# Decay attention, one head behind the other, with its projections in three fp32r passes placed between the heads' work

## The chip, the cores and the metric

One core of one Trainium2 chip runs the whole program. The metric is the device time of one launch in microseconds (us), as the median of several runs. TensorE (PE, with its weight loads as PEld) does the matmuls, VectorE (DVE) and ScalarE (ACT) the elementwise work, GpSimd (POOL) and SyncE (SP) help; each engine takes its own instructions in order, and waits on semaphores that the others raise.

## What is computed

The program is a small network on 512 tokens of width 1024: two layers of a first kind (two feed-forward blocks and a mixer each), then a second block with sparse attention, a mixture of experts, decay attention ("hgrn") and a second mixture of experts. The change touches decay attention alone. Of the reference, cut:

```python
def hgrn2_mixer(h, lower_bound, w_in, out_gain, w_out):
    q, f, i, g = jnp.split(h @ w_in, ...)             # 1024 columns each
    q = jax.nn.silu(q)                                # 8 heads of 128 keys
    log_f = log(lb + (1 - lb) * sigmoid(f));  k = 1 - exp(log_f);  v = i
    def chunk_step(S, xs):
        cum = jnp.cumsum(lf_c, axis=2)
        rel = where(causal, cum[t] - cum[s], -inf)
        attn = einsum('bhtd,bhsd,bhtsd->bhts', q_c, k_c, exp(rel))
        o = attn @ v_c + (q_c * exp(cum)) @ S
        S = exp(last) * S + (k_c * exp(last - cum))^T @ v_c
    o = rms_norm(o, out_gain) * jax.nn.silu(g)
    return o @ w_out
```

`x` becomes `x + gate * y`, with `h` the modulated norm of `x`.

## The kernel before

`P` is 128, `TT` 4 token tiles of 128, `KT` 8 tiles of the width, `HG` 8 heads. The stage (`hgrn`, L1631 on) opens with `Norm`: statistics of `x`, 32 transposes on PE, and eight evacuations shared by ACT and DVE into `hT`. It is in plain fp32, 4 MB of SBUF tiles hold all heads at once, and the phases run for all heads before the next phase begins:

- Projections of forget gates and queries (L1720): 16 tiles of 512 columns, eight matmuls each, in six PSUM banks (`Banks`). The weights come through `Ring`, two slots of 2 MB, and go to PE as they are. ACT and DVE evacuate (`evacuate`, L595 and L597); DVE scales the gates (L1875 to L1877), ACT takes the logarithm (L1820), DVE the running sums over 128 tokens (L1881), ACT the silu of the queries.
- Levels. The causal 128x128 square of each head and token tile is put together from eight patterns: the diagonal, and for each block size 1, 2, ... 64 the pairs in which the key is in the first and the query in the second half of a block of twice that size. Such a unit (head, size) is: two subtractions on DVE (`gaps`, L1893 and L1894, 256 columns each), an exponential on ACT (L1828), two multiplications by keys and queries on DVE (L1902, L1903), four 128x128 matmuls on PE (L1744) and a predicated copy into `att` on DVE (L1910). There are 64 units; those of the diagonals come first. PE's order puts one tile of the value and gate projections (L1729, eight matmuls) ahead of every four units. The decayed product has four slots (`M`), a level two PSUM banks.
- States and outputs: key decays for all heads (L1919, L1836, L1924), 32 transposes of keys (L1753), query decays (L1928), then by token tile the state increments (L1774), the states (L1947, L1953) and the outputs (L1781, L1785), their squares (L1936, L1937).
- The end: root, normalisation and gate (L1965, L1967), 32 transposes (L1793), evacuation with the gain, and the output projection (L1807, 64 matmuls), whose results are added to `x` (L1080, L1081).

Other stages of the same program already use three passes in fp32r, a rounded format: `split_matmul` (L209 to L213) multiplies high by high, high by low and low by high parts. A weight half of 1 MB is split by ACT (the high part, a copy to fp32r, as L2180 in the experts stage) and DVE (the low part, a subtraction, L2268), and `ModulatedSplitNorm` (L250) splits `h` in the same way.

Of the kernel before, what the change touches and what calls it, by code (L numbers as in the profile page):

```python
# [1630 lines left out]
def hgrn(chip):  # L1631
# [5 lines left out]
    units = [(h, None) for h in range(HG)] + [(h, b) for h in range(HG) for b in LEVELS[1:]]  # L1637
    U = len(units)
    with Scope(nc, "hgrn") as s:
        banks = Banks(s, 6)  # L1640
        level_ps = [s.ps(f"level{i}", [P, SEQ]) for i in range(2)]

        FQ, VG, KK, GROW, OC, OT, OUT = 0, 16, 32, 40, 42, 50, 58
        a = s.sb("region_a", [P, 4096])
        b = s.sb("region_b", [P, 4096])
        norm = Norm(chip, s, banks.ps[0:4], a[:, :], b[:, :])
        norm.allocate(s)
        qT = s.sb("qT", [P, HG, SEQ])
        kT = s.sb("kT", [P, HG, SEQ])
        cum = s.sb("cum", [P, HG, SEQ])  # L1650
        v = s.sb("v", [P, TT, DM])
        g = s.sb("g", [P, TT, DM])
        scratch = a[:, :].rearrange("p (h t) -> p h t", h=HG)
        att = b[:, :].rearrange("p (h c t) -> p h c t", h=HG, c=TT)
        kk = a[:, :].rearrange("p (c d) -> p c d", c=TT)
        o_tok = cum[:, :, :].rearrange("p h t -> p (h t)").rearrange("p (c d) -> p c d", c=TT)
        o_heads = cum[:, :, :].rearrange("p h t -> p (h t)").rearrange("p (u e) -> p u e", e=P)
        squares = kT[:, :, :].rearrange("p h t -> p (h t)").rearrange("p (u e) -> p u e", e=P)
        cum_ch = cum[:, :, :].rearrange("p h t -> p (h t)").rearrange("p (u t) -> p u t", t=P)
        counts = [4, 8, 12, 16, 20, 24, 28, 32, OUT + 4, OUT + 8]  # L1660
        ring = Ring(s, 2, [(dram["hgrn_w"][i], 4096, n) for i, n in enumerate(counts)], banks.computed)
        masks = s.sb("masks", [P, len(LEVELS), P], I32)
        keep = s.sb("keep", [P, SEQ])
        M = [s.sb(f"decayed{i}", [P, SEQ]) for i in range(4)]
        state = [s.sb(f"state{i}", [P, HG, P]) for i in range(2)]
# [3 lines left out]
        gate_row = s.sb("gate_row", [P, DM])  # L1669
        diag = s.sb("diag", [P, KT, P])  # L1670
        small_loaded, own_v = s.sem("small_loaded"), s.sem("own_v")
        lb_diff, lb_exp = s.sem("lb_diff"), s.sem("lb_exp")
        f_scaled, f_log, q_silu, g_silu, cum_ready = s.sem("f_scaled"), s.sem("f_log"), s.sem("q_silu"), s.sem("g_silu"), s.sem("cum_ready")
        gaps_ready, decays_ready, m_ready = s.sem("gaps_ready"), s.sem("decays_ready"), s.sem("m_ready")
        level_done, level_taken, att_zeroed = s.sem("level_done"), s.sem("level_taken"), s.sem("att_zeroed")
        cum_exp, last_gaps, last_exp, q_decayed, k_decayed = s.sem("cum_exp"), s.sem("last_gaps"), s.sem("last_exp"), s.sem("q_decayed"), s.sem("k_decayed")
        decay_ready, state_done, state_ready = s.sem("decay_ready"), s.sem("state_done"), s.sem("state_ready")
        o_var, o_rstd, o_normed, diag_ready, x_added = s.sem("o_var"), s.sem("o_rstd"), s.sem("o_normed"), s.sem("diag_ready"), s.sem("x_added")
        block = s.block()

        outputs = {}
        for m in range(HG):
            outputs[FQ + 2 * m] = [piece(cum[:, m, :], func=ACT.Sigmoid), piece(kT[:, m, :], func=ACT.Sigmoid, scale=-1.0)]
            outputs[FQ + 2 * m + 1] = [piece(qT[:, m, :])]
            outputs[KK + m] = [piece(kk[:, m // 2, 512 * (m % 2):512 * (m % 2) + 512])]
            outputs[OC + m] = [piece(o_tok[:, m // 2, 512 * (m % 2):512 * (m % 2) + 512])]
            outputs[OT + m] = [piece(qT[:, m, :], scale=chip.gain("hgrn_out_gain_2", 0))]
# [24 lines left out]
        def _(pe):  # L1712
# [10 lines left out]
            for step in range(16):  # L1723
# [8 lines left out]
                for u in range(4 * step, 4 * step + 4):  # L1732
# [8 lines left out]
                    if u >= 2:  # L1741
                        pe.wait_ge(level_taken, u - 1)
# [988 lines left out]
```

## Time and profile before

| | us |
|---|---|
| median of 3 runs (3726.86 to 3735.7) | 3733.4 |
| profiled execution | 3737.17 |
| its span | 3735.2 |
| decay attention in it, 2891.3 to 3354.0 | 462.7 |

Busy over the whole span: PE 3360.6 us (90%), PEld 2599.2, DVE 2025.7 (54%), ACT 1338.0 (36%), POOL 159.2 (4%). The table says that PE is the busiest engine overall, but one stage among many is changed, and what bounds that stage must be read from its own windows: how long each phase takes, how much of it PE, DVE and ACT are busy, and which engine's records stand ahead of the idle time. A busy share below 100% on every engine at once means that they wait for each other in turn.

### The profile page before, as it was taken

The page shows a single profiled execution, that of the slowest core. Times are in us where ns is not written, and L with a number is a line of the kernel's source. Part 1 is how long each engine was busy: PE and PEld are TensorE (multiplying, and loading weights), DVE is VectorE, ACT ScalarE, POOL GpSimd, SP SyncE. Part 2 cuts the span into 40 slices and gives each one's busy share as a digit, 9 for nine tenths or more (in the row PEclk, how much of TensorE's full clock was granted, in tenths as well). Part 3 has the DMA queues.
Part 4 walks back from the last instruction along what each step waited for, and adds up shares of the span by engine and source line. Part 5 has one row for each costly group of instructions (what it writes and reads, how often), then busy time and mean ns, then how long its engine had stood idle before and what let it go on. Part 6 is the DMA issues. An engine that isn't in the chain of part 4 may idle for free. (4 is left out here: it accounts for less than half of the span.)

```text
span 3735.2 us, 39164 instructions
## 1 busy us (share of the span) xinstructions
PE 3360.6 (90%) x15110; PEld 2599.2 (70%) x15110; DVE 2025.7 (54%) x2724; ACT 1338.0 (36%) x1734; POOL 159.2 (4%) x194
## 2 busy tenths in 40 slices
PE   7999988999989999888999798888996988778995
PEld 6888756788878887567888585457885444547884
DVE  4554435555455544255554544545987246746886
ACT  3222223322132222243222323635885121305884
POOL 0000000000000000000000003410100000000100
PEclk9999999999999999999999797997998999997998
DMA  4331320433143323304331411017995210107995
GB/s 187 152 128 63 128 102 1 180 136 134 56 161 140 133 73 118 112 1 163 152 135 56 146 46 68 1 51 294 415 415 228 90 68 23 46 22 276 415 415 228
DMA packets 85490, 537.55 MB, mean 144 GB/s; under 512 B 9232, under 2 KB 10128, under 8 KB 37088
## 3 DMA queue, kind: packets, MB, share of 16 engines
q1 hardware_dynamic: 72912, 489.95, 33.9%
q0 software_dynamic: 7824, 28.84, 2.0%
q10 hardware_dynamic: 4608, 16.78, 1.1%
q8 instruction: 95, 1.56, 0.2%
q14 instruction: 51, 0.42, 0.0%
HBM read 512.43 MB, written 32.02 MB: 146 GB/s over the span
## 5 line engine op out<-in xcount | busy, mean ns | idle before, releaser
L211 PE MATMUL ffn_gate_up<-ffn_h_high,ffn_gate_up_high 128*128 128x512 f32 x1408 | 548.4, 389 | 7.1 <-DVE ffn_h_low L245 7.1
L213 PE MATMUL ffn_gate_up<-ffn_h_high,ffn_gate_up_low 128*128 128x512 f32 x1408 | 548.0, 389 | 0.0
L212 PE MATMUL ffn_gate_up<-ffn_h_low,ffn_gate_up_high 128*128 128x512 f32 x1408 | 547.9, 389 | 0.0
L2268 DVE TENSOR_TENSOR moe_low<-moe_raw,moe_high 128x2048 fp32r<-128x2048 f32 x192 | 433.9, 2287 | 38.6 <-ACT moe_high L2180 38.4
L451 ACT ACTIVATE ffn_silu_gate<-ffn_gate_up 128x512 f32<-128x512 f32 x88 | 52.7, 598 | 971.6 <-PE ffn_gate_up L213 971.6
L2180 ACT ACTIVATE moe_high<-moe_raw 128x2048 fp32r<-128x2048 f32 x192 | 364.4, 1917 | 18.9 <-PE moe_bank L213 18.9
L482 DVE TENSOR_TENSOR ffn_product<-ffn_silu_gate,ffn_gate_up 128x512 f32<-128x512 f32 x88 | 60.5, 688 | 568.8 <-ACT ffn_silu_gate L451 568.8
L211 PEld LDWEIGHTS ffn_gate_up<-ffn_h_high,ffn_gate_up_high 128*128 128x128 f32 x1408 | 264.3, 188 | 63.2 <-DVE ffn_h_low L245 8.4
L213 PEld LDWEIGHTS ffn_gate_up<-ffn_h_high,ffn_gate_up_low 128*128 128x128 f32 x1408 | 264.3, 188 | 55.2
L212 PEld LDWEIGHTS ffn_gate_up<-ffn_h_low,ffn_gate_up_high 128*128 128x128 f32 x1408 | 264.3, 188 | 55.1
L506 DVE SCALAR_TENSOR_TENSOR x_tok<-ffn_down,x_tok 128x512 f32<-128x512 f32 x352 | 232.9, 687 | 94.6 <-PE ffn_down L213 93.2
L211 PE MATMUL ffn_down<-ffn_down_high,ffn_hid_high 128*128 128x512 f32 x704 | 282.5, 401 | 1.6 <-DVE x_tok L506 1.6
L212 PE MATMUL ffn_down<-ffn_down_low,ffn_hid_high 128*128 128x512 f32 x704 | 281.0, 399 | 0.0
L213 PE MATMUL ffn_down<-ffn_down_high,ffn_hid_low 128*128 128x512 f32 x704 | 280.6, 399 | 0.0
L470 DVE TENSOR_TENSOR ffn_gate_up_low<-ffn_raw_gate_up,ffn_gate_up_high 128x2048 fp32r<-128x2048 f32 x88 | 201.5, 2289 | 74.1 <-ACT ffn_gate_up_high L440 74.0
L211 PE MATMUL moe_bank<-moe_high,moe_xT_high 128*128 128x512 f32 x512 | 207.0, 404 | 4.3 <-DVE moe_xT_low L2275 4.3
L213 PE MATMUL moe_bank<-moe_high,moe_xT_low 128*128 128x512 f32 x512 | 201.2, 393 | 0.0
L212 PE MATMUL moe_bank<-moe_low,moe_xT_high 128*128 128x512 f32 x512 | 200.8, 392 | 0.0
L440 ACT ACTIVATE ffn_gate_up_high<-ffn_raw_gate_up 128x2048 fp32r<-128x2048 f32 x88 | 168.2, 1912 | 39.8 <-DMA ffn_raw_gate_up<-in_ffn_gate_up 39.8
L211 PEld LDWEIGHTS ffn_down<-ffn_down_high,ffn_hid_high 128*128 128x128 f32 x704 | 135.0, 192 | 33.6 <-DVE x_tok L506 2.4
L213 PEld LDWEIGHTS ffn_down<-ffn_down_high,ffn_hid_low 128*128 128x128 f32 x704 | 134.7, 191 | 32.0
L212 PEld LDWEIGHTS ffn_down<-ffn_down_low,ffn_hid_high 128*128 128x128 f32 x704 | 135.0, 192 | 31.2
(488 smaller groups left out, 5645.2 us busy)
## 6 DMA issues: line engine op xcount, KB each, us to landing
moe_raw<-in_moe_w SPq DMA_DIRECT2D x192, 1024.0 KB, 7.8
ffn_raw_gate_up<-in_ffn_gate_up SPq DMA_DIRECT2D x88, 1024.0 KB, 6.5
ffn_ada_w<-in_ada_w SPq DMA_DIRECT2D x32, 1536.0 KB, 6.6
ffn_raw_down<-in_ffn_down SPq DMA_DIRECT2D x88, 512.0 KB, 3.3
mixer_w_raw<-in_mix_w SPq DMA_DIRECT2D x24, 1024.0 KB, 5.2
hgrn_ring<-in_hgrn_w SPq DMA_DIRECT2D x10, 2048.0 KB, 7.6
moe_y<-moe_y ACTq DMA_DIRECT2D x32, 512.0 KB, 9.4
nsa_w_raw<-in_nsa_w SPq DMA_DIRECT2D x14, 1024.0 KB, 5.3
```

Of the source, the lines that this page charges most:

```text
L211: pe.matmul(out, lhsT[0], rhs[0], start=first, stop=False)
L212: pe.matmul(out, lhsT[0], rhs[1], start=False, stop=False)
L213: return pe.matmul(out, lhsT[1], rhs[0], start=False, stop=last)
L440: act.activation(gu_high[slot][:, :, :, :], raw_gu[slot][:, :, :, :], ACT.Copy).then_inc(gu_high_ready, 1)
L451: act.activation(silu_gate[slot][:, :], gate_up_ps[2 * slot][:, :], ACT.Silu).then_inc(silu_done, 1)
L470: dve.tensor_tensor(gu_low[slot][:, :, :, :], raw_gu[slot][:, :, :, :], gu_high[slot][:, :, :, :].bitcast(FP32), ALU.subtract).then_inc(gu ...
L482: dve.tensor_tensor(product[slot][:, :], silu_gate[slot][:, :], gate_up_ps[2 * slot + 1][:, :], ALU.mult)\
L506: dve.scalar_tensor_tensor(out=xs, in0=down_ps[o % 4][:, :], scalar=0.5, in1=xs, op0=ALU.mult, op1=ALU.add).then_inc(x_added, 1)
L2180: act.activation(high[n % SPLITS][:, :, :], raw[n % RAWS][:, :, :], ACT.Copy).then_inc(high_ready, 1)
L2268: dve.tensor_tensor(low[n % SPLITS][:, :, :], raw[n % RAWS][:, :, :], high[n % SPLITS][:, :, :].bitcast(FP32), ALU.subtract)\
```

## The change

The stage is written anew, with the same mathematics:

- All projections, those of the output too, go by `split_matmul`. `h` is split by `ModulatedSplitNorm`. Each of the 20 halves of weights (1 MB) is loaded into one of two raw buffers, split by `make_high` on ACT and `make_low` on DVE into one of two pairs. Matmuls of 128x512: 320 in fp32 before, 960 in fp32r now. A `part` is the work of one half of the contraction (four of eight tiles) for one bank: 12 matmuls. Four banks are open per group of 512 columns.
- Units are ordered head by head. The first two groups (values of heads 0 to 3; gates and queries of heads 0 and 1) are projected ahead; then 72 ticks follow, and 48 parts of the next six groups are spread over the first 64 of them, none in every fourth. In tick n each engine's program has: `gaps(n)`, `multiply(n-1)`, `keep_level(n-3)` on DVE, `decays(n)` on ACT, at most one part and `level(n-2)` on PE. Per head, from tick 8h+8 on, come query and key decays, three transposes of keys, three state increments, the states and the outputs; the sums of squares are taken by ACT (four `Square` with accumulation). At given ticks `make_high`, `make_low`, the gates, silus, logarithms and scans of later heads are put in.
- `gaps` is one subtraction of 512 columns instead of two of 256, `multiply` one product of 512 instead of two, `decays` two exponentials of 256 (one with scale -1) instead of one of 512. `M` has three slots, not four.
- At the end, normalisation and gate are one operation for each head and tile (32 of 128 columns); each token tile is transposed, split by ACT and DVE, and its first part of the output projection may start when that tile is ready.

```diff
-    units = [(h, None) for h in range(HG)] + [(h, b) for h in range(HG) for b in LEVELS[1:]]
+    units = [(h, b) for h in range(HG) for b in LEVELS]
+    GROUPS = [("v", 0), ("fq", 0), ("fq", 1), ("fq", 2), ("v", 1), ("fq", 3), ("g", 0), ("g", 1), ("out", 0), ("out", 1)]
+    FIRST, PARTS = 2, 48
+    def tick_of(part):
+        return -(-(part + 1) * U // PARTS) - 1
...
-            ring.fill(sp, 0, 2)
+            for n in range(2 * len(GROUPS)):
+                if n >= 2:
+                    sp.wait_ge(w_ready, n - 1)
+                sp.dma_start(raw[n % 2][:, :], dram["hgrn_w"][COLUMNS[kind] + i, :, ...]).then_inc(w_loaded[n % 2], 16)
...
-                    for k in range(KT):
-                        last = pe.matmul(bank[:, :], w[:, k, m * P:(m + 1) * P], norm.hT[:, k, :], ...)
+            def part(gi, half, m):
+                if m == 0:
+                    pe.wait_ge(w_ready, n + 1)
+                if half == 0 and gi >= 1:
+                    pe.wait_ge(taken[m], gi)
+                if kind == "out" and gi == len(GROUPS) - 2 and half == 0:
+                    pe.wait_ge(oT_ready, 2 * m + 2)
+                for i in range(4):
+                        last = split_matmul(pe, banks[m][:, :], ...)
...
+            for tick in range(U + 8):                                      # TensorE
+                while p < PARTS and tick_of(p) <= tick:
+                    part(FIRST + p // 8, p // 4 % 2, p % 4)
+                if 0 <= tick - 2 < U:
+                    level(tick - 2)
+                h, at = divmod(tick - 8, 8)
+                    if at == 2: turn_keys(h)
+                    if at == 4: increments(h)
+                    if at == 6: output(h)
...
+            for tick in range(U + 8):                                      # ScalarE
+                    decays(tick)
+                    if n + 2 < 20 and tick == done_tick(n // 2, n % 2, 3) + 1: make_high(n + 2)
+                        if tick == done_tick(gi, 1, 2) + 1: forget_gates(gi)
+                        if tick == done_tick(gi, 1, 3) + 1: queries(gi)
+                        if tick == done_tick(gi, 1, 3) + 3: logs(i)
+                if at == 7: query_decay(h + 1)
+                    if at == 1: key_decay(h)
+                    if at == 3: take_keys(h)
+                    if at == 7: take_output(h)
+                if tick == U + 2:
+                        act.activation(g[:, t, :], g[:, t, :], ACT.Silu)
...
+            for tick in range(U + 8):                                      # VectorE
+                    gaps(tick); multiply(tick - 1); keep_level(tick - 3)
+                    if at == 0: query_decay(h)
+                    if at == 1: key_decay(h)
+                    if at == 5: add_states(h)
+                    if n + 2 < 20 and tick == done_tick(n // 2, n % 2, 3) + 2: make_low(n + 2)
...
+            def gaps(u):
+                if w >= 3:
+                    dve.wait_ge(level_done, 8 * ((w - 3) // 7) + (w - 3) % 7 + 2)
...
+            for t in range(TT):
+                for h in range(HG):
+                    dve.scalar_tensor_tensor(out=o_tok[:, t, h * P:(h + 1) * P], ..., op0=ALU.mult, op1=ALU.mult).then_inc(o_normed, 1)
+                if t > 0:
+                    take_turned(t - 1)
```

## Rows read from the trace of the kernel before

**Rows 1.** Busy time by stretch of the stage: length, busy of each engine, clock, DMA.

```profile
2891.30:2904.90 13.60, 6.72 (x32) 5.91 (x32) 9.66 (x19) 8.96 (x13) 0.84 (x1) 0.57 0.92 364
2904.90:3014.90 110.00, 109.95 (x257) 48.76 (x258) 18.12 (x36) 14.49 (x25) 2.67 (x1) 1.00 0.16 58
3014.90:3236.60 221.70, 179.46 (x769) 111.12 (x767) 141.44 (x308) 46.64 (x75) 0.00 (x0) 0.98 0.13 48
3236.60:3281.00 44.40, 27.82 (x208) 27.12 (x208) 37.40 (x69) 21.59 (x33) 0.00 (x0) 0.81 0.00 1
3281.00:3354.00 73.00, 62.27 (x160) 30.25 (x160) 23.57 (x28) 2.75 (x4) 0.00 (x0) 0.91 0.00 0
```

**Rows 2.** The ring's matmuls: records, ns min/median/max, first and last start (us), forms.

```profile
L1720 PE MATMUL hgrn_bank<-hgrn_region_a,hgrn_ring x256: 592/592/667, 2904.9 to 3014.5; 128*128 128x512 f32 x128
L1729 PE MATMUL hgrn_bank<-hgrn_ring,hgrn_region_a x256: 592/592/1061, 3014.9 to 3229.5; 128*128 128x512 f32 x128
L1807 PE MATMUL hgrn_bank<-hgrn_ring,hgrn_qT x128: 592/592/667, 3297.3 to 3351.9; 128*128 128x512 f32 x128
```

**Rows 3.** Timeline, experts stage, fp32r passes: start (us), us, engine, line, operation.

```profile
2850.24 0.39 PE L211 MATMUL moe_bank<-moe_high,moe_xT_high 128*128 128x512 f32 x1
...
2852.73 0.39 PE L213 MATMUL moe_bank<-moe_high,moe_xT_low 128*128 128x512 f32 x1
```

**Rows 4.** Timeline of one period in the levels: start (us), us; brackets hold idle and releaser.

```profile
3069.92 7.03 PE L1729 MATMUL hgrn_bank<-hgrn_ring,hgrn_region_a 128*128 128x512 f32 x16
...
3076.79 1.95 PE L1744 MATMUL hgrn_level<-hgrn_decayed 128*128 128x128 f32 x16
3077.88 0.73 DVE L1910 COPY_PREDICATED hgrn_region_b<-hgrn_masks,hgrn_level 128x512 f32<-128x512 int32 x1 [4.61 <-PE hgrn_level L1744]
...
3083.42 7.03 PE L1729 MATMUL hgrn_bank<-hgrn_ring,hgrn_region_a 128*128 128x512 f32 x16
```

**Rows 5.** Groups by line (L1445: sparse attention): busy us, mean ns, idle, releaser.

```profile
L1910 DVE COPY_PREDICATED hgrn_region_b<-hgrn_masks,hgrn_level 128x512 f32<-128x512 int32 x64 | 46.4, 725 | 76.1 <-PE hgrn_level L1744 76.0
L1903 DVE TENSOR_TENSOR hgrn_decayed<-hgrn_decayed,hgrn_qT 128x256 f32<-128x256 f32 x56 | 23.8, 426 | 1.9
L1928 DVE TENSOR_TENSOR hgrn_qT<-hgrn_qT,hgrn_decayed 128x512 f32<-128x512 f32 x8 | 4.9, 681 | 0.0
L1953 DVE SCALAR_TENSOR_TENSOR hgrn_state<-hgrn_state,hgrn_decay,hgrn_level 128x128 f32<-128x128 f32 x16 | 4.4, 343 | 0.8 <-PE hgrn_level L1774 0.6
L1828 ACT ACTIVATE hgrn_decayed<-hgrn_decayed 128x512 f32<-128x512 f32 x56 | 35.3, 630 | 169.3 <-DVE hgrn_decayed L1894 169.3
L1781 PE MATMUL hgrn_bank<-hgrn_v,hgrn_region_b 128*128 128x128 f32 x64 | 11.7, 284 | 0.0
L1445 ACT ACTIVATE nsa_k_tok<-nsa_k_tok,nsa_neg_max 128x256 f32<-128x256 f32 x32 | 16.0, 500 | 10.4 <-DVE nsa_neg_max L1585 10.4
```

**Rows 6.** The splits of the experts' weight halves: count, ns min/median/max, first and last start.

```profile
L2180 ACT ACTIVATE moe_high<-moe_raw x192: 1897/1915/1932, 2531.1 to 3685.2; 128x2048 fp32r<-128x2048 f32 x192
L2268 DVE TENSOR_TENSOR moe_low<-moe_raw,moe_high x192: 2280/2285/2295, 2545.0 to 3687.2; 128x2048 fp32r<-128x2048 f32 x192
```

**Rows 7.** Timeline: ACT changes its function table ahead of the gate's silus.

```profile
3257.86 1.28 ACT L1844 ACT_TABLE_LOAD   x1
3259.16 3.90 ACT L1844 ACTIVATE hgrn_g<-hgrn_g 128x1024 f32<-128x1024 f32 x4
```

**Rows 8.** Timeline, sparse attention stage: its split norm, and a projection after idle time.

```profile
2098.51 1.89 ACT L712 ACTIVATE nsa_w_high<-nsa_w_raw 128x2048 fp32r<-128x2048 f32 x1
...
2109.34 0.77 PE L211 MATMUL nsa_bank<-nsa_h_high,nsa_w_high 128*128 128x512 f32 x1
...
2464.28 0.76 PE L211 MATMUL nsa_bank<-nsa_w_high,nsa_oT_high 128*128 128x512 f32 x1 [4.86 <-issue]
...
2469.50 0.40 PE L211 MATMUL nsa_bank<-nsa_w_high,nsa_oT_high 128*128 128x512 f32 x1
```

**Rows 9.** DMA issues: count, KB each, median us from issue to landing.

```profile
hgrn_ring<-in_hgrn_w SPq DMA_DIRECT2D x10, 2048.0 KB, 7.6
```

More of the change, by code:

```diff
@@ L1639, in hgrn @@
     with Scope(nc, "hgrn") as s:
-        banks = Banks(s, 6)
+        banks = [s.ps(f"bank{i}", [P, 512]) for i in range(4)]
         level_ps = [s.ps(f"level{i}", [P, SEQ]) for i in range(2)]
[L1643 to L1649, printed above, removed]
@@ L1661, in hgrn @@
-        ring = Ring(s, 2, [(dram["hgrn_w"][i], 4096, n) for i, n in enumerate(counts)], banks.computed)
-        masks = s.sb("masks", [P, len(LEVELS), P], I32)
+        att = s.sb("att", [P, 2, TT, P])
+        M = [s.sb(f"decayed{i}", [P, SEQ]) for i in range(3)]
+        kk = s.sb("kk", [P, TT - 1, P])
+        state = s.sb("state", [P, TT - 1, P])
+        decay_of = s.sb("decay_of", [P, SEQ])
+        squares = s.sb("squares", [P, P])
+        masks = s.sb("masks", [P, len(LEVELS) - 1, P], I32)
@@ new lines, in level @@
+            def level(u):
+                h, size = units[u]
+                if size is None:
+                    pe.wait_ge(cum_ready, h + 1)
+                    left, right = k_of(h), q_of(h)
+                else:
+                    pe.wait_ge(m_ready, index(h, size) + 1)
+                    left = right = slot(u)
+                if u >= 2:
+                    pe.wait_ge(level_taken, u - 1)
+                for c in range(TT):
+                    last = pe.matmul(level_ps[u % 2][:, tokens(c)], left[:, tokens(c)], right[:, tokens(c)], start=True, stop=True)
+                last.then_inc(level_done, 1)
@@ L1788, in _ @@
[L1788 to L1809 removed]
+                last.then_inc(row_done, 1)
@@ new lines, in queries, with logs @@
+            def queries(gi):
+                pair = GROUPS[gi][1]
+                for i in range(2):
+                    h, m = 2 * pair + i, 2 * i + 1
+                    act.wait_ge(computed, 4 * gi + m + 1)
+                    if h >= 4:
+                        act.wait_ge(o_done, h - 3)
+                    act.activation(q_of(h), banks[m][:, :], ACT.Silu).then_inc(taken[m], 1)
+            def logs(pair):
+                for h in range(2 * pair, 2 * pair + 2):
+                    act.wait_ge(f_scaled, h + 1)
+                    act.activation(cum[:, h % 4, :], cum[:, h % 4, :], ACT.Ln).then_inc(f_log, 1)
```

599 lines of the change are left out of this document (353 added, 246 removed).

## The prediction

> **What bounds the kernel now.** The rest of the program is untouched, so only the stage's 462.7 us can move. I read it by stretches first [rows 1]: norm 13.6 us, gate and query projections 110.0, levels with the value and gate projections 221.7, key decays to the outputs' statistics 44.4, end 73.0. Their PE column is the thing to see: PE is busy 109.95 of 110.0 in the second stretch and 179.5 of 221.7 in the third, so matmul time is the limit there, with 42.2 us of waiting on top. In the fourth PE is busy 27.8 of 44.4 with DVE at 37.4: there DVE leads. In the fifth 62.3 of 73.0 is PE again, after a serial normalisation.
>
> Then the size of the matmul work. 128 matmuls of 128x512 (256 records) run from 2904.9 to 3014.9 [rows 1, 2], 0.859 us each. All 320 are 275 us of the 462.7. In the experts stage the same shape in fp32r starts at 2850.24 and, eleven matmuls later, at 2852.73 [rows 3]: 0.2264 us, thus 0.679 for three passes. (The 0.39 us in the row is duration and overlaps the next.)
>
> Then how the third stretch loses its 42 us. A period runs from one projection tile to the next, 3069.92 to 3083.42, 13.5 us; within it PE does eight matmuls in one go (7 us) while DVE, having used up its four slots, stands idle 4.6 us; then PE waits for DVE's products [rows 4]. DVE's idle time before the predicated copies is 76.0 us in all, released by PE [rows 5]. Both engines wait in turn.
>
> **The change part by part.** The sum follows PE from 2891.3 on.
>
> *Norm and first split, 13.6 becomes 18.4.* ACT now splits a weight half before it evacuates, and each of the eight tiles of `h` costs DVE two operations in a row instead of one in every second tile. The sparse attention stage has the same chain: from its first weight split (2098.51) to its first projection matmul (2109.34) 10.8 us [rows 8]. The split starts when the weights have landed; the two first halves are 2 MB together, which took 7.6 us [rows 9]. Statistics, memset and masks hide below it. 7.6 + 10.8 = 18.4, bounds 15 and 21.
>
> *The first two groups, 45.* 16 parts of 12 matmuls: 192 x 0.2264 = 43.5. After idle time the first 12 matmuls of a projection took 5.22 us (2464.28 to 2469.50) instead of 2.72 [rows 8], so up to 2.5 more; I take 1.5. Weight splits are hidden: a half costs ACT 1.92 and DVE 2.29 [rows 6], 4.2 in sequence, and must be ready one half of PE work (10.9 us) after its buffer is freed. The SP queue waits for `w_ready` before each load, with only later loads behind it. Then PE has parts for tick 1 to 3 but waits for the first scan and product behind logarithms, splits and table loads: 2.
>
> *The 64 ticks, PE's own work 213.* 48 parts are 576 x 0.2264 = 130.4. A level is half of the 1.95 us that 16 records take [rows 4], 0.98; 62 of them until the last part are 61. Per head 13 more 128x128 matmuls: at the levels' 0.245 they are 3.2, at the 0.37 of the output matmuls (11.7 us for 32, [rows 5], partly at the low clock) 4.8; seven heads, near the first, 22. Semaphore switches between parts and levels are in the waiting below.
>
> *DVE beside it, about 180.* Before, a unit cost four operations of 256 columns (0.42 to 0.43) and a copy of 0.73. Now it is two of 512, 0.68 each [rows 5] with about 0.08 of overlap, and the copy: about 1.85, for 64 units some 115 with the diagonals left out. The shape of `multiply` (two strided runs in one access) is in no row; from 0.68 up to the two old operations, 0.85; I take 0.68, the row of its element count. Twelve low splits add 27, per head query and key decays and three states (three at 0.68, three at 0.34, plus own waits) 3.2, thus 24 for seven and a half heads; gates, scans and takes of the six later groups 20. Near 83% of PE's 213. *ACT beside it, about 140.* Two exponentials of 256: the row of that width has 0.50 with two accumulations and a pointer, half of the 512 one is 0.32 [rows 5]; I take 0.4, 45 in all; high splits 23, gates and takes 18, per head decays, squares and the output copy 4.5, 34; table changes 23. Two thirds of 213.
>
> *Table changes.* The old order needs seven or eight in the stage, the new one six per group of gates in the loop (sigmoid, exponential, silu, exponential, logarithm, exponential), 18 more. One took 1.28 us, the next activation began 1.30 after its start [rows 7]: 23 us. They stand in the ticks where a high split and six gate activations stand too. The Trainium skill ("ScalarE: Activation LUTs", section "What ACT_TABLE_LOAD costs") gives 2.66 us for a change, a drain of 1.38 included, and tells to batch activations by table set, which this change undoes. By that figure ACT would have 25 us more, which its third of free time still covers in the mean; the sum would rise by at most 12 where they bunch. The trace has no room for the drain (1.30), so the row is taken.
>
> *What waits and what is queued behind it.* A level on PE waits for the product of its unit, and the next part is queued behind it; `gaps` waits until the slot three units back was read by PE, with DVE's copies and splits behind. Each engine may therefore be about one tick ahead. A PE tick is 3.7 with a part and 1.0 without, 3.3 in the mean with the heads; DVE's is 1.85, but 4 to 5.7 where a low split and gate scaling fall in it, ACT's 0.8, but 4.5 and 6.5 in the two ticks in a row where gates and queries come. `queries` of head 5 waits for `output(1)`, at the end of its own tick on PE, with the next exponentials behind. I give 3 us per group of gates (9), and 0.7 per low split (8): 17, 8% of 213. Bounds: 0 (every burst covered), and 42, what PE idles in this stretch now [rows 1].
>
> *From the last part to the root, 44.4 becomes 18.* The phases over eight heads are gone; what is left is head 7: two levels 2, decays 2 (largely beside them), but the gate's silus (1.3 + 3.9, [rows 7]) now stand ahead of ACT's copy of the turned keys, 5.2; copy 0.5, increments 0.7, states 1.3, outputs 1.7, four squares and a copy 2.6, statistics and root with a table load 2; waits and low clock 2. Bounds 15 and 24.
>
> *The end, 73.0 becomes 54.* Before, everything was normalised and turned before the first of 64 x 0.859 = 55 us. Now a tile's eight operations of 128 columns (0.28 to 0.34, [rows 5]) are 2.5; with transposes, split and the next tile's normalisation between, the first part starts after 6.2, the following 3.7 apart, the fourth, whose banks are freed last, after 16. Then its own 2.7, 12 parts of 2.72 (32.6), two additions 1.6, slow start 1. The splits of the last two halves (4.2 each) fit in 10.9. Bounds 51 and 59.
>
> Sum: 18.4 + 45 + 2 + 213 + 17 + 18 + 54 = 367.4, against 462.7: 95.3 less. The span 3735.2 becomes 3639.9, the profiled time 3737.2 becomes 3641.9; the median of the runs stands 3.8 below the profiled time, so the median is 3733.4 - 95.3 = 3638.1.
>
> **The rivals.**
>
> *Forecast, 0.60:* PE sets the pace with a moderate loss, 3638, own range 3626 to 3650.
>
> *Every burst is covered, 0.14:* DVE has 17% and ACT a third of slack. No waiting in the ticks: 3621. Against it: three engines in fixed order with a lead of one tick.
>
> *They still wait in turn, 0.19:* the bursts hit harder, and PE loses the 42 us that it loses now, 25 more than in the sum: 3663. For it: DVE's 83% leaves little room to catch up, and unmeasured shapes may be dearer (multiply at 0.85 adds 10 us of DVE). In stretches with more idle PE time the granted clock was 0.81 [rows 1], the lower of two levels (1.2 and 2.4 GHz) for part of it, which makes waiting dearer.
>
> *Slower, 0.04:* one lap of the ring of slots sets each tick. With three slots instead of four, a unit's gaps 0.68, exponentials 0.8, product 0.68, the part ahead of its level 2.7, level 0.98 and copy 0.73 come one after the other, 6.6 us a tick; 62 ticks are 409 instead of 230, the median 3817. It decides from 5.2 us a tick on (3.7 + 95/62). Against it: slots for three units allow three such chains at once, a lap of 6.6 thus 2.2 per unit, below PE's tick.
>
> *Nothing gained, 0.03:* the three passes don't run at 0.2264 here or ticks come to 5.0 to 5.4 by some mix. Were a pass a third of 0.859, it would cost 57 us more, 3695; only with slow ticks besides it comes to no change.
>
> **How the numbers follow.** About 0.3% (11 us) is what a measurement of this kernel can tell from no change. The first three cases are faster: 0.60 + 0.14 + 0.19, and half of the last one's 0.03 with a little: 0.94. Same 0.02, slower 0.04. The range must leave out at most 2 in 10: it takes the second and third case with the bounds of norm, tail and end (about 8 either way): 3621 - 8 = 3613, 3663 + 9 = 3672.
>
> **What the profile would show.** Matmuls of the projections at 0.226 us from start to start, 960 of them. Right: 64 ticks in 225 to 235 us, PE over 88% busy there, DVE 75 to 85%, the stage 360 to 375 us. The wait view should name DVE's `multiply` (level waits) ahead of `computed` waits; ACT with some 26 table loads. The first projection matmul near 18 us from the start, the last part to the root near 18, the end near 54. Wrong would be: ticks over 4.2 us in the mean, DVE over 95% busy (then its new shapes cost more), a copy or exponential that holds PE for over 5 us in each group, or a clock below 0.9 in the loop.

## The result and the profile after

The changed kernel takes 3638.8 us in the median (3633.2 to 3647.2), the kernel before 3731.5 in runs on the same chip: 0.9754 of its time, 95% interval 0.9731 to 0.9776. The forecast was 3638. In a later series it took 3639.2 (0.9738, interval 0.9720 to 0.9755). The profiled execution of the changed kernel has a span of 3637.2 us.

The stage now runs from 2886.9 to 3253.3 us of the span, 366.4 us against 462.7 before [rows 1]; 367.4 were forecast. These are the stretches of the changed kernel that answer to [rows 1]: norm and first split, first two groups, ticks up to the last part, up to the statistics' root, up to the first part of the output projection, and the rest. Columns: stretch, length, busy time and number of instructions of PE, weight loads, DVE, ACT and POOL, granted clock, DMA share, GB/s.

```profile
2886.90:2905.10 18.20, 8.30 (x32) 6.12 (x33) 15.09 (x25) 12.15 (x16) 0.00 (x0) 0.50 0.60 213
2905.10:2950.50 45.40, 45.40 (x191) 36.72 (x190) 18.50 (x25) 13.74 (x13) 0.95 (x1) 0.97 0.29 93
2950.50:3172.50 222.00, 212.33 (x1230) 184.29 (x1229) 175.45 (x260) 130.55 (x271) 0.00 (x0) 0.98 0.18 58
3172.50:3191.70 19.20, 10.71 (x64) 9.24 (x62) 9.41 (x14) 12.13 (x23) 0.00 (x0) 0.73 0.17 55
3191.70:3205.20 13.50, 6.63 (x32) 5.58 (x33) 12.44 (x38) 5.40 (x9) 0.00 (x0) 0.62 0.00 0
3205.20:3253.30 48.10, 46.54 (x194) 37.10 (x192) 17.06 (x20) 4.77 (x4) 0.00 (x0) 0.97 0.00 0
```

PE is busy 96% of the ticks, against 81% of the third stretch of [rows 1], with DVE at 79% and ACT at 59%. What PE still waits for in the ticks (engine, tile and line, released by; us in total, times, longest):

```profile
PE hgrn_kk_bank L1791 <- ACT hgrn_kk L1909: 5.9, 3, 2.7
PE hgrn_level L1777 <- DVE hgrn_att L2036: 1.4, 2, 0.8
PE hgrn_bank L211 <- ACT hgrn_kq L1872: 1.1, 1, 1.1
PE hgrn_bank L211 <- ACT hgrn_kq L1881: 0.9, 1, 0.9
PE hgrn_level L1777 <- DVE hgrn_decayed L2026: 0.3, 1, 0.3
```

These are 9.6 us, all that the ticks' row leaves beside PE's busy time (222.0 - 212.3). The groups of instructions (busy us, mean ns, idle before them and its releaser), for the copies, products, gaps and exponentials of [rows 5]:

```profile
L2036 DVE COPY_PREDICATED hgrn_att<-hgrn_masks,hgrn_level 128x512 f32<-128x512 int32 x56 | 41.4, 739 | 9.7 <-PE hgrn_level L1777 9.7
L2026 DVE TENSOR_TENSOR hgrn_decayed<-hgrn_decayed,hgrn_kq 128x512 f32<-128x512 f32 x56 | 38.3, 684 | 0.7 <-ACT hgrn_decayed L1893 0.7
L2019 DVE TENSOR_TENSOR hgrn_decayed<-hgrn_cum 128x512 f32<-128x512 f32 x56 | 38.2, 684 | 24.9 <-PE hgrn_level L1777 24.9
L1892 ACT ACTIVATE hgrn_decayed<-hgrn_decayed 128x256 f32<-128x256 f32 x56 | 23.8, 425 | 89.6 <-DVE hgrn_decayed L2019 89.5
```

The product over two strided runs takes 684 ns, as its element count said. The 76 us that DVE idled before its copies in [rows 5] are 9.7 now, with 24.9 more before the gaps.

The same program profiled once more (`changed_again` below) has the ticks in 219.0 us at a granted clock of 1.00 instead of 222.0 at 0.98, and the stage in 363.4. PE's list of waits is the same in both, to within 0.1 us, so all 3 us are PE's busy time (209.3 against 212.3). Stage lengths are therefore compared with 363.4 to 366.4, and a difference under 3 us is not read unless the clocks are equal.

### The profile page after: what moved, and what is told of

Its sections match the earlier page's. It is cut to its first block and busy times, and to the rows that moved or that the text cites. A ratio compares the mean times of both kernels' runs of the same rounds, so it can differ in the third digit from the quotient of the medians.

```text
span 3637.2 us, 40038 instructions
## 1 busy us (share of the span) xinstructions
PE 3302.4 (91%) x15422; PEld 2651.7 (73%) x15422; DVE 2043.3 (56%) x2647; ACT 1421.7 (39%) x1916; POOL 156.5 (4%) x194
```

## The experiments

| kernel | median us (range) | ratio to before, 95% | stage us | ticks us | PE busy in ticks |
|---|---|---|---|---|---|
| changed kernel | 3638.8 (3633.2–3647.2) | 0.9754 (0.9731–0.9776) | 366.4 | 222.0 | 212.3 |
| e1_parts_between | 3624.8 (3621.0–3629.1) | 0.9715 (0.9693–0.9738) | 358.4 | 219.1 | 209.4 |
| e2_fp32 | 3681.5 (3676.1–3683.4) | 0.9862 (0.9836–0.9889) | 406.6 | 241.9 | 239.4 |
| e3_two_passes | 3585.8 (3582.3–3589.5) | 0.9607 (0.9582–0.9633) | 319.7 | 203.4 | 178.3 |
| e4_more_dve | 3657.3 (3656.9–3662.8) | 0.9807 (0.9780–0.9833) | 377.5 | 232.3 | 214.4 |
| e5_two_slots | 3690.1 (3686.6–3693.9) | 0.9876 (0.9860–0.9893) | 424.1 | 275.7 | 229.4 |
| e5_four_slots | 3634.3 (3630.9–3638.0) | 0.9733 (0.9717–0.9750) | 363.1 | 219.0 | 210.8 |
| e6_layout | 3642.3 (3638.5–3649.3) | 0.9758 (0.9739–0.9776) | 366.1 | 221.8 | 212.1 |
| e8_keys_first | 3629.9 (3628.9–3636.6) | 0.9722 (0.9704–0.9741) | 359.4 | 215.4 | 208.4 |
| changed_again | 3639.2 (3629.2–3640.6) | 0.9738 (0.9720–0.9755) | 363.4 | 219.0 | 209.3 |
| e7_aligned | 3629.9 (3626.4–3630.6) | 0.9719 (0.9704–0.9733) | 361.9 | 219.1 | 208.6 |
| e9_all | 3622.1 (3614.1–3625.2) | 0.9697 (0.9681–0.9714) | 346.5 | 212.3 | 206.1 |
| e10_all_and_down | 3613.0 (3596.5–3622.0) | 0.9684 (0.9668–0.9701) | 346.6 | – | – |

Edits are against the changed kernel. The kernel before stood at 3731.5 us beside the first row, and at 3733.0, 3733.3 and 3733.8 beside the three series of four kernels that follow, each on one chip. Only `e7_aligned`, `e9_all` and `e10_all_and_down` have the changed kernel (`changed_again`) in their own series. The medians of the others are set beside the first row, from another chip, and are the weaker figure (14 us less in the first experiment, where its stage is 5 to 8 shorter).

**The end: parts between the transposes.** Of the terms of the sum only the end fell outside its bounds: 13.5 + 48.1 = 61.6 us against 54 (51 to 59). The timeline of the changed kernel, PE and DVE from the first normalisation on (start, us, engine, line, operation, in brackets idle time before it and releaser), shows why:

```profile
3193.95 0.66 PE L1840 MATMUL hgrn_kk_bank<-ident,hgrn_o_tok 128*128 128x128 f32 x4 [2.54 <-DVE hgrn_o_tok L2145]
...
3196.57 0.74 DVE L2139 SCALAR_TENSOR_TENSOR hgrn_oT_low<-hgrn_o_bank,cols,hgrn_oT_high 128x512 fp32r<-128x512 f32 x1
3196.80 1.09 PE L1840 MATMUL hgrn_kk_bank<-ident,hgrn_o_tok 128*128 128x128 f32 x4 [1.67 <-DVE hgrn_oT_low L2139]
...
3200.22 1.09 PE L1840 MATMUL hgrn_kk_bank<-ident,hgrn_o_tok 128*128 128x128 f32 x4 [1.48 <-DVE hgrn_oT_low L2139]
...
3203.64 1.09 PE L1840 MATMUL hgrn_kk_bank<-ident,hgrn_o_tok 128*128 128x128 f32 x4 [1.47 <-DVE hgrn_oT_low L2139]
3204.52 1.06 PE L1840 MATMUL hgrn_o_bank<-ident,hgrn_o_tok 128*128 128x128 f32 x4
...
3205.23 0.78 PE L211 MATMUL hgrn_bank<-hgrn_w_high,hgrn_oT_high 128*128 128x512 f32 x1
```

The operands of the first part are split at 3197.31 (3196.57 and 0.74), yet it starts at 3205.23: in PE's program the transposes of all four tiles stand ahead of it, 3.4 us apart from the second tile on, each pair waiting for DVE's low half. Putting the parts between them is the experiment.

```diff
+            last_group = len(GROUPS) - 2
             for t in range(TT):
...
                     last.then_inc(o_turned, 1)
-            for gi in range(len(GROUPS) - 2, len(GROUPS)):
-                for half in range(2):
-                    for m in range(4):
-                        part(gi, half, m)
+                if t > 0:
+                    part(last_group, 0, t - 1)
+            part(last_group, 0, TT - 1)
+            for m in range(4):
+                part(last_group, 1, m)
+            for half in range(2):
+                for m in range(4):
+                    part(last_group + 1, half, m)
```

> The changed kernel, with one edit at its end: on TensorE the first half part of the output projection for token tile t-1 is queued right behind the transposes of tile t, instead of all four behind the transposes of all four tiles. In the profile of the changed kernel the first part starts 13.5 us after the first normalisation (3191.7 to 3205.2) and the projection takes 48.1 us, 61.6 in all; the sum had 54, with parts from 6.2 us on. Theory (PE's own queue order was mis-read: parts stand behind the last tile's transposes): the first part moves to about 7 us and the two stretches together to 53 to 56, so 6 to 8 us less than the changed kernel, about 3631. Rival (the low clock after the idle stretch and VectorE's pace of 3.4 us a tile eat it): the parts run at 0.43 us a matmul between the transposes and delay these; 60 us or more in all, less than 2 us gained.

The end of the experiment's kernel:

```profile
3191.50:3198.20 6.70, 2.68 (x16) 2.47 (x17) 6.68 (x23) 2.68 (x5) 0.00 (x0) 0.76 0.00 0
3198.20:3248.00 49.80, 48.22 (x210) 38.94 (x208) 22.82 (x36) 7.28 (x8) 0.00 (x0) 0.96 0.00 0
```

The first part starts 6.7 us after the first normalisation, as expected, and the end takes 56.5 us: 5.1 less than 61.6 and inside the sum's bounds (51 to 59), but just above the 53 to 56 and short of the 6 to 8 us that this run was expected to give. A part of what the rival named is there too: the first part begins at the low clock (granted 0.50 from 3198.2 to 3201.5) and takes 4.5 us, to 3202.70, instead of 2.7. The medians differ by 14 us, more than the stage's 5 to 8; the intervals of the two ratios overlap, so the medians do not say that more was gained than the stage shows. That PE's queue order is the main cause of the mis-sized term is shown.

**What the three passes alone are worth.** Order and stage as changed, but each projection matmul of this stage in one fp32 pass over the high parts (the low parts are made and not used), and then, in a second kernel, in two of the three passes (high by high, high by low). The other stages keep their three passes; the cuts show one of the two calls.

```diff
+def one_fp32(pe, out, lhsT, rhs, first, last):
+    return pe.matmul(out, lhsT[0].bitcast(FP32), rhs[0].bitcast(FP32), start=first, stop=last)
...
-                        last = split_matmul(pe, banks[m][:, :], ...
+                        last = one_fp32(pe, banks[m][:, :], ...
```

```diff
+def two_passes(pe, out, lhsT, rhs, first, last):
+    pe.matmul(out, lhsT[0], rhs[0], start=first, stop=False)
+    return pe.matmul(out, lhsT[0], rhs[1], start=False, stop=last)
...
-                        last = split_matmul(pe, banks[m][:, :], ...
+                        last = two_passes(pe, banks[m][:, :], ...
```

> The changed kernel with one plain fp32 matmul of the high parts instead of three fp32r passes in this stage (the products with the low parts are left out, the splits are still made). It keeps the new order and takes the cheaper passes away. 320 matmuls at 0.859 us instead of 3 x 0.2333: 0.159 us more each. Theory (PE sets the pace everywhere in the stage): all of it shows, 51 us, about 3690; then of the 95 us gained about half belongs to the passes and half to the order. Rival (in the ticks the engines wait for each other and the matmul price is partly covered): the 192 in the ticks cost at most half of their 30.5 us, 35 us or less, 3674 or below.

> The changed kernel with two of the three fp32r passes in this stage (the product of the low part of the stationary operand is left out). 320 x 0.2333 = 75 us of PE work less, 30 outside the ticks and 45 in them. Theory (PE sets the pace in the ticks at 212 of 222 us, VectorE is next with 175.5): outside all of it goes, in the ticks PE falls to 168, below VectorE, so the ticks stop at 185 to 200 instead of 177; about 3639 - 30 - 30 = 3580. Rival A (nothing but PE counts): 3564. Rival B (the bound in the ticks is the waiting in turn): the ticks stay above 210, 3600 or more.

```profile
2970.30:3212.20 241.90, 239.39 (x1041) 146.46 (x1040) 174.99 (x260) 131.72 (x273) 0.00 (x0) 1.00 0.16 53
```

```profile
2940.60:3144.00 203.40, 178.27 (x1038) 154.76 (x1037) 174.05 (x260) 128.45 (x262) 0.00 (x0) 0.94 0.20 66
```

These are the ticks, fp32 first, two passes second. With fp32 matmuls the stage is 406.6 us, 40 to 43 more than the changed kernel's; the median is 43 more and still 52 under the kernel before in its series. It lies between the two cases expected (3690, and 3674 or below). Outside the ticks the dearer matmuls show in full (9.6 us in the first two groups, 11 at the end), in the ticks 20 to 23 of 30.5: PE's idle time falls from 9.7 to 2.5 us and covers most of the rest. So of the 96 us by which the stage shrank 40 to 43 come with the passes, and 56 with all else that was rewritten. By stretches, against [rows 1], that is 35 less for projections and levels together (296.9 against 331.7) and 25 less for the phases over eight heads (18.9 against 44.4), with 5 more for the norm and nothing at the end (72.5 against 73.0). Head by head, placing of parts and larger operations were changed together, and no run separates them.

In the other direction PE's work is cut by 44.6 us in the ticks (192 passes at 0.2325) and they shrink by 16 to 19 only, to 203.4, where 185 to 200 were expected: PE waits 25 us instead of 10, and its busy time is 178.3 and not the 168 expected, at a clock of 0.94. DVE is 86% busy. Outside the ticks the projections lose all of their 30 us (15.0 and 14.7). The median fell by 53 us (3585.8, expected about 3580). From here on a faster PE gives back less than half of its gain in the ticks.

**How much room DVE has.** The gaps of each of the 56 units are computed twice, once into an unused buffer.

```diff
+                dve.wait_ge(spared, w)
+                dve.tensor_tensor(spare[:, :].rearrange(...), blocks, ..., ALU.subtract).then_inc(spared, 1)
                 dve.tensor_tensor(slot(u)[:, :].rearrange(...), blocks, ..., ALU.subtract).then_inc(gaps_ready, 1)
```

> The changed kernel with the subtraction of each of the 56 decayed units made twice on VectorE, the first one into a spare tile: 56 x 0.60 to 0.68 = 34 to 38 us more VectorE work in the ticks, whose busy time there goes from 175 to about 211 of 222. Theory (PE sets the pace and VectorE has 20% of slack): most is covered, the ticks grow by 5 to 15 us, 3644 to 3654. Rival (each tick is a chain through VectorE): they grow by the full 34 to 38, 3675.

```profile
2957.60:3189.90 232.30, 214.39 (x1230) 185.44 (x1229) 206.77 (x315) 128.21 (x260) 0.00 (x0) 0.98 0.17 55
```

DVE's busy time rises by 31 us to 89%, the ticks by 10 to 13 (5 to 15 were expected), the stage by 11 to 14, the median by 18.5, to 3657.3, just over the 3644 to 3654 expected. By the ticks some three fifths of the added work are hidden. DVE is not what sets the pace, but it is no longer free either.

**The ring of slots.** Two and four slots for the decayed products, instead of three.

```diff
-        M = [s.sb(f"decayed{i}", [P, SEQ]) for i in range(3)]
+        M = [s.sb(f"decayed{i}", [P, SEQ]) for i in range(2)]
...
-            return M[index(h, size) % 3]
+            return M[index(h, size) % 2]
...
-                if w >= 3:
-                    dve.wait_ge(level_done, 8 * ((w - 3) // 7) + (w - 3) % 7 + 2)
+                if w >= 2:
+                    dve.wait_ge(level_done, 8 * ((w - 2) // 7) + (w - 2) % 7 + 2)
```

> Two slots for decayed products instead of three; the same work. My theory of the ticks (each engine may be about one tick ahead, and a part of 2.8 us on PE covers the chain gap 0.68, exponentials 0.8, product 0.68 of the next unit): with two slots gap n waits for level n-2, so only the product of unit n-1, behind that gap, is left for the one part in between. The 16 ticks without a part lose about 1.5 us each (24), and those where a split, a take or a state stands on DVE another 1 us each (16): median 3660 to 3685, 25 to 45 us over the changed kernel, and PE's waits in the wait view name the decayed products first. Rival, ring by the mean: a lap of 6.6 us over two slots is 3.3 us a tick, under PE's 3.5, so the time stays within 10 us of 3639. Rival, one lap per tick: 62 x 6.6 = 409 us of ticks, median 3817.

> Four slots instead of three; the same work. The wait view of the changed kernel has DVE's gaps waiting 24.9 us for levels, but PE's own waits for decayed products are 0.3 us and those for copies 1.4 us. My theory: DVE's wait for the slots costs nothing, since PE hardly waits for DVE; the time stays within 4 us of 3639. Rival: the 24.9 us are on the path, and a fourth slot gives back 10 us or more, 3629 or less.

The ticks with two slots, and a place in them (PE and DVE, some rows left out):

```profile
2954.00:3229.70 275.70, 229.44 (x1231) 197.05 (x1230) 174.09 (x256) 127.45 (x258) 0.00 (x0) 0.92 0.14 46
```

```profile
3017.61 1.05 PE L1777 MATMUL hgrn_level<-hgrn_decayed 128*128 128x128 f32 x8
3018.77 0.69 DVE L2019 TENSOR_TENSOR hgrn_decayed<-hgrn_cum 128x512 f32<-128x512 f32 x1 [2.20 <-PE hgrn_level L1777]
3019.38 0.68 DVE L2026 TENSOR_TENSOR hgrn_decayed<-hgrn_decayed,hgrn_kq 128x512 f32<-128x512 f32 x1
3019.98 0.72 DVE L2036 COPY_PREDICATED hgrn_att<-hgrn_masks,hgrn_level 128x512 f32<-128x512 int32 x1
...
3020.85 2.05 PE L1777 MATMUL hgrn_level<-hgrn_decayed 128*128 128x128 f32 x8 [2.19 <-DVE hgrn_att L2036]
...
3022.55 0.77 PE L211 MATMUL hgrn_bank<-hgrn_h_high,hgrn_w_high 128*128 128x512 f32 x1
```

Two slots cost 51 us in the median, 58 to 61 in the stage. The mechanism is the forecast's, one wait with the rest of the engine queued behind it: DVE's gap waits for the level at 3017.61, its product and copy stand behind the gap, and the next level waits 2.19 us for that copy. I expected the products at the head of PE's waits; it is the copies (32.8 us). The size was expected at 25 to 45 us (3660 to 3685), and 3690.1 is above. PE's idle time in the ticks rises from 9.7 to 46.3 us, 37 more, which is inside; the rest is 4 us in the stretch behind the ticks, and 17 because the same matmuls keep PE busy for 229.4 us instead of 212.3, at a granted clock of 0.92. The eight records of the level after the wait take 2.05 us where those before it took 1.05, and the first pass of the next part 0.77. Waiting was paid once as waiting and, by half as much again, in the clock. That half is no constant: with two passes PE idled 15 us more than in the changed kernel, at a clock of 0.94, and was busy 11 to 14 us longer than its work accounts for (178.3 against 212.3 - 44.6, or 209.3 - 44.6). The ring's mean (a lap over two slots, no change) and one lap per tick (3817) both fall.

Four slots change nothing that can be read: stage 363.1, ticks 219.0, and a median 4.5 us lower from another chip, its interval overlapping both of the changed kernel's. DVE's waits before its gaps, 24.9 us with three slots, vanish from its list, those before its copies rise from 8.4 to 25.4 us, and PE's waits remain: DVE idles elsewhere, and PE waits for it hardly longer than before (1.9 us for copies, 0.3 for products).

**Keys first on ACT.** PE's largest wait in the ticks is for ACT's copy of the turned keys, which stands behind weight splits, gates and queries in ACT's order. One of its three waits in the changed kernel:

```profile
2987.54 1.89 ACT L1856 ACTIVATE hgrn_w_high<-hgrn_w_raw 128x2048 fp32r<-128x2048 f32 x1
2989.45 1.28 ACT L1881 ACT_TABLE_LOAD   x1
2990.75 1.08 ACT L1881 ACTIVATE hgrn_kq<-hgrn_bank 128x512 f32<-128x512 f32 x2
2991.72 0.50 ACT L1909 ACTIVATE hgrn_kk<-hgrn_kk_bank 128x384 f32<-128x384 f32 x1
...
2992.27 0.94 PE L1791 MATMUL hgrn_kk_bank<-hgrn_v,hgrn_kk 128*128 128x128 f32 x6 [2.70 <-ACT hgrn_kk L1909]
```

In the 2.70 us that PE waits, ACT changes its table (1.28), takes two silus (1.08) and copies the keys (0.50).

```diff
                     decays(tick)
+                if tick >= 8 and (tick - 8) % 8 == 3 and (tick - 8) // 8 < HG:
+                    take_keys((tick - 8) // 8)
...
-                    if at == 3:
-                        take_keys(h)
```

> On ACT, the copy of a head's turned keys (0.5 us) is put right behind the tick's two exponentials, ahead of splits, gates, queries and logarithms that fall in the same tick. PE's increments wait for this copy: 5.9 us in three waits, the longest 2.7, in the ticks of the changed kernel, and 3.8 in the last head's phase, which has nothing ahead of it but the silus and stays. Theory: these waits are on the path: 4 to 6 us less, 3633 to 3635, and the three waits gone from PE's list. Rival: PE, the sooner through, waits for the next thing (products or query copies, delayed by 0.5 us each), and the time stays within 2 us.

```profile
2949.10:3164.50 215.40, 208.44 (x1228) 181.58 (x1227) 174.98 (x260) 130.45 (x270) 0.00 (x0) 1.00 0.18 59
```

```profile
PE hgrn_bank L211 <- ACT hgrn_kq L1881: 4.0, 3, 1.5
PE hgrn_level L1777 <- DVE hgrn_att L2036: 1.4, 2, 0.8
PE hgrn_bank L211 <- ACT hgrn_kq L1872: 1.1, 1, 1.1
```

The keys' wait is gone from the ticks, and the one for the evacuation of the banks grew from 0.9 to 4.0. The ticks are 3.6 us shorter than the changed kernel's at the same clock (219.0, and 219.1 in `e1_parts_between`), 2.7 of it waiting; the stage is 4 us shorter than 363.4. Moving a 0.5 us copy is worth the lower end of the 4 to 6 us expected. The median is 9 us lower, from another chip, and the stage does not bear out that much.

**Places of the operands.** The passes run 0.2325 us apart in this stage, where 0.2264 had been read from [rows 3]. First only the order of the four split buffers was changed, as the sparse attention stage has it.

```diff
-        w_high = [s.sb(f"w_high{i}", [P, 4, 512], F32R) for i in range(2)]
-        w_low = [s.sb(f"w_low{i}", [P, 4, 512], F32R) for i in range(2)]
+        w_high, w_low = zip(*[[s.sb(f"w_{part}{i}", [P, 4, 512], F32R) for part in ("high", "low")] for i in range(2)])
```

> Only the places of the four split weight buffers in SBUF change: high and low of a half side by side, as in the sparse attention stage, instead of both highs first. The 960 fp32r passes run 0.2326 to 0.2337 us apart in this stage and 0.2269 in the sparse attention stage. Theory: the places make the difference; the pitch becomes 0.227 and the time 5 to 6 us less, 3633. Rival: the pitch has another cause; it stays at 0.233 and the time within 3 us of 3639.

No effect: 0.2323 to 0.2326 apart, stage 366.1. The order of the buffers is not the cause. Their start addresses, as the built program lists them, gave the next theory; its edit is one line, and the last kernel has it in the feed-forward stages too.

```diff
+        s.sb("pad", [P, 96])
         raw = [s.sb(f"w_raw{i}", [P, 2048]) for i in range(2)]
```

> One unused buffer of 384 bytes per partition ahead of the weights' buffers, nothing else. In the program's list of places, `h` and `oT` begin 32 bytes past a multiple of 512 and the split weights 160 past one. In the sparse attention stage and in the experts both begin at 32, in the gate and up projections of the feed-forward stages both at 160, and there the passes are 0.2266 to 0.2270 us apart; in the down projections one is at 32, the other at 160, and there they are 0.2323 apart as in this stage. Theory: the distance of 128 bytes between the two operands, modulo 512, makes the difference; with the weights at 32 the pitch in this stage becomes 0.227, and 960 x 0.0056 are 5.4 us less: ratio to the changed kernel of the same call 0.9985. Rival: a coincidence; the pitch stays at 0.2323 and the ratio at 1.

> The changed kernel once more, as a measure for the others of this call: 0.975 of the kernel before, pitch 0.2325 in the stage, ticks 222 us.

Two passes of the same kind, 24 passes apart (the rows between them left out), in the changed kernel:

```profile
2931.64 0.40 PE L211 MATMUL hgrn_bank<-hgrn_h_high,hgrn_w_high 128*128 128x512 f32 x1
...
2937.24 0.40 PE L211 MATMUL hgrn_bank<-hgrn_h_high,hgrn_w_high 128*128 128x512 f32 x1
```

And in the kernel with the unused buffer:

```profile
2932.11 0.39 PE L211 MATMUL hgrn_bank<-hgrn_h_high,hgrn_w_high 128*128 128x512 f32 x1
...
2937.55 0.39 PE L211 MATMUL hgrn_bank<-hgrn_h_high,hgrn_w_high 128*128 128x512 f32 x1
```

5.60 / 24 = 0.2333 and 5.44 / 24 = 0.2267 us (over the 87 passes from 2929.72 to 2949.95 of `changed_again` the pitch is 0.2325). It is not the weights' place by itself: in the feed-forward stages of the changed kernel `h` and the gate and up weights both begin at 160, and nine passes there are 0.2267 us apart:

```profile
299.77 0.39 PE L211 MATMUL ffn_gate_up<-ffn_h_high,ffn_gate_up_high 128*128 128x512 f32 x1
...
301.81 0.39 PE L211 MATMUL ffn_gate_up<-ffn_h_high,ffn_gate_up_high 128*128 128x512 f32 x1
```

That moving one operand against the other changes the pitch is shown. What it does to the time is less clear: where PE is alone the stage gains what was expected (first two groups 45.4 to 44.7, end 47.9 to 47.0), in the ticks no gain can be read (219.1 against 219.0), and the stage is 1.5 to 4.5 us shorter, where 5.4 were expected. The ratios, 0.9719 and 0.9738, have overlapping intervals. The Trainium skill ("SBUF — State Buffer", section "Operand start alignment") asks for starts at a multiple of the element size, says that this is about legality and not speed, and that its runs timed nothing; both places are legal by it.

**All together.** Parts between transposes, keys first, four slots, the buffer ahead of the weights, and the gates' silus one tick later, behind the last head's keys (`if tick == U + 3` instead of `U + 2`): in the changed kernel PE waits 3.8 us for those keys in the tail, with ACT at its silus. Then also the feed-forward stages' buffer.

> Five edits together: parts between transposes, keys first on ACT, four slots, the weights at 32 bytes past a multiple of 512, and the gates' silus one tick later, behind the copy of the last head's keys. Were they additive by the profiles: 5 (between transposes) + 6.6 (ticks 222.0 to 215.4 with keys first) + 3.8 (PE's wait for the last keys) + 5.4 (places) + 0 to 3 (slots) = 21 to 24 us less than the changed kernel: 3615 to 3618. Rival: gains lie on each other, above all keys first, slots and silus, whose waits are next to one another: 12 to 16 less, 3623 to 3627.

> The five edits, and 384 unused bytes in the feed-forward stages too, so that the down projections' operands both begin at 32. They have 2112 passes of 0.2323 us. Theory (places): 0.0056 less each, 11.8 us, and PE is over 96% busy there, so 10 to 12 us less than the five edits. Rival: the places mean nothing: no change against the five edits.

```profile
2954.00:3166.30 212.30, 206.10 (x1227) 180.98 (x1226) 174.78 (x259) 130.94 (x272) 0.00 (x0) 1.00 0.19 60
3166.30:3182.60 16.30, 11.34 (x59) 9.96 (x59) 9.41 (x15) 11.73 (x20) 0.00 (x0) 0.66 0.20 65
3182.60:3189.30 6.70, 5.01 (x24) 4.34 (x23) 6.68 (x23) 2.90 (x5) 0.00 (x0) 0.50 0.00 0
3189.30:3237.60 48.30, 46.80 (x210) 38.48 (x208) 22.86 (x37) 7.24 (x8) 0.00 (x0) 0.97 0.00 0
```

The five edits give 17 us less than the changed kernel of the same series, in the median and in the stage (346.5 against 363.4): ticks 6.7, tail 3.0, end 6.5, first groups 0.7. I had expected 21 to 24 if they add up, and 12 to 16 if the gains lie on each other; 17 is neither. My sum had started from the ticks at 222.0, the execution at the lower clock, and 3 us of it were that. Of the 18 to 21 that are left, 1 to 4 did not come. At the end they add up (5.1 and about 1 for the pitch, against 6.5); how the ticks' 6.7 divide among keys, slots and places isn't separated.

In the last kernel the down projections' pitch falls too. In `changed_again` 45 passes go from 303.71 to 314.17 us (0.2324); now:

```profile
299.95 0.39 PE L211 MATMUL ffn_down<-ffn_down_high,ffn_hid_high 128*128 128x512 f32 x1
...
308.79 0.39 PE L211 MATMUL ffn_down<-ffn_down_high,ffn_hid_high 128*128 128x512 f32 x1
```

8.84 us for 39 passes are 0.2267. The effect of the places is confirmed in a second stage. The kernel's median, 3613.0, is 9 us under that of the five edits, where 10 to 12 were expected; its runs spread over 25 us, and the intervals overlap, so the time by itself settles little. It is the fastest of the versions that compute everything: 0.9684 of the kernel before.

## Why the prediction was right, and where it was not

*Norm and first split*, 18.4 forecast, 18.2 measured. *First two groups*, 45: 45.4, though by 192 x 0.2325 = 44.6 and 0.8 of slow start, not 43.5 and 1.5.

*Ticks*, 2 + 213 + 17 = 232: 222.0, below the 225 to 235 that were to show it right. PE's own work of 213 is 212.3, from two errors that cancel: the passes are 576 x 0.2325 = 133.9 instead of 130.4, so the levels and heads are 78.4 instead of 83. The waiting, the 2 at the start included, was the step that was mis-sized, 9.7 against 19; its main term is inside its bounds of 0 and 42. Its places were partly wrong: the wait view was to name DVE's `multiply` first, but bursts of gates and splits hardly reach PE through the products (0.3 us), rather through the 0.5 us copy of the keys that stands behind them on ACT (5.9 us). I had named what waits for `multiply` and `computed`, and not who waits for `take_keys`. The loads were 175 and 131 us for DVE and ACT, forecast 180 and 140. DVE's terms, as they stand, add up to 186, and its 115 for the units was not worked out right: 56 units at 1.85 are 104. The rows have 117.9 for them, because busy time counts both of two records that overlap. The product at 684 ns took the lower of its bounds, the exponentials 409 and 425 ns where 400 were taken.

*Table changes*: 26 in the stage as counted, ten of them ahead of the exponentials:

```profile
L1892 ACT ACT_TABLE_LOAD x10 | 12.8, 1283 | 0.2
...
3176.27 1.28 ACT L1968 ACT_TABLE_LOAD   x1
3177.57 3.90 ACT L1968 ACTIVATE hgrn_g<-hgrn_g 128x1024 f32<-128x1024 f32 x4
```

All take 1.28 us. In the tail the silus start 1.30 after the load, as [rows 7] had it, and without the drain that the Trainium skill ("ScalarE: Activation LUTs", section "What ACT_TABLE_LOAD costs") adds. The 12 us that its figure would have put on the sum are not there. No run takes the table changes away, so what they cost the ticks stays open; the rows of the keys' wait show that they are not free, one of them being nearly half of 2.70 us on PE.

*Last part to root*, 18: 19.2, of them 3.8 the wait for the last keys behind the silus, which the step had.

*The end*, 54 (51 to 59): 61.6. The step "the first part starts after 6.2" was wrong: it started after 13.5. I took the condition of the wait (this tile's split is ready) for the order of the program, which has all transposes ahead. With the order of the step the end takes 56.5. Of the 2.5 us that are left over 54 the step's own arithmetic has a part: the first part after 6.2 and three more 3.7 apart put the fourth at 17.3, not 16.

That the sum lands 1.0 us from the stage's length is luck: 10.0 us too much for the ticks stand against 7.6 too little for the end and 1.2 for the tail. Outside the stage the span changed by 1.7 us net, without an edit there (4.4 less ahead of it, 2.7 more behind). What was right is the mechanism of the likeliest case: PE sets the pace with a moderate loss. Against "every burst covered", 3621: it has 215 us for the ticks and no waiting, and PE waits 9.6 us in the changed kernel; they came to 215.4 once the keys were first, with 7 us of PE's waits left. Against "they still wait in turn", 3663: two slots show what that looks like, 46 us of idle PE in the ticks. "One lap per tick" is refuted by the two slots too, whose ticks take 4.3 us in the mean.

## What to carry to other kernels

When engines run fixed programs side by side, price a wait by what is queued behind it, and look for the small copy behind large work: moving one 0.5 us copy ahead gave back 3.6 us in the ticks, while a fourth buffer, which took the longest waits off DVE's list, gave nothing, because PE hardly waited for DVE. A condition on a semaphore says when a step may run, the order of its engine's program when it will; read both before a start time is written down. And when waiting goes up on PE, add the clock: half as much again with two slots, and 0.7 to 0.9 of the added waiting with two passes.

## What the runs showed of the hardware that was not expected

- The pitch of 128x512 fp32r passes depends on where the two operands begin: 0.2267 us where both start at the same offset modulo 512 bytes (both at 32, or both at 160), 0.2325 where they are 128 bytes apart; an unused buffer took it from the one to the other in two stages. Other distances weren't tried, so neither the period nor the mechanism is known.
- 37 us more of idle time on PE went with 17 us more of busy time for the same matmuls, at a granted clock of 0.92 instead of 0.98 (two slots).
- Two executions of one program differ by 3 us in one stage, with the same waits, at granted clocks of 0.98 and 1.00. Over these kernels, at about equal waits, PE's busy time in the ticks is 212.3 and 212.1 us at 0.98, 210.8 at 0.99 (four slots), 209.3 and 209.4 at 1.00.
